# Ups first, downs last: the feed-forward values of a float32 two-block kernel take a detour through HBM

## The reference

```
def conv_ffn(h, up, conv_w, conv_b, down):
    hid = causal_dwconv(h @ up, conv_w, conv_b)
    gate, val = jnp.split(hid, 2, axis=-1)
    return (jax.nn.gelu(gate) * val) @ down

h = rms_norm(x, pre_ffn_norm)
y = conv_ffn(h, up, conv_w, conv_b, down)
x = x + rms_norm(y, post_ffn_norm)
```

## Time and profile before

| what | value |
|---|---|
| median of 3 runs | 2734.21 us (2734.03 to 2734.27) |
| profiled execution: span, first to last instruction | 2732.1 us |
| what lies around the span, as the runs have it | 2.1 us (2734.2 - 2732.1) |
| TensorE matmul busy | 2721.5 us, 100% of the span, 14368 matmuls |
| DVE busy | 1481.2 us, 54% |
| ACT busy | 844.7 us, 31% |
| POOL busy | 192.2 us, 7% |
| mean busy share of the DMA engines | 27.6% on SP's queue, 2.9% on POOL's |
| HBM read / written | 268.41 MB / 16.78 MB |

### The profile page before, as it was taken

The page is one execution under the profiler, slowest core; times in us unless marked ns, Lnnn a source line. Parts: engine busy times, 40 slices in busy tenths (PEclk is TensorE's granted clock), DMA queues, the critical chain, the costliest instruction groups (busy, mean ns, idle before and its releaser), DMA issues.

```text
span 2732.1 us, 34402 instructions
## 1 busy us (share of the span) xinstructions
PE 2721.5 (100%) x14368; PEld 2235.1 (82%) x14368; DVE 1481.2 (54%) x1764; ACT 844.7 (31%) x917; POOL 192.2 (7%) x193
## 2 busy tenths in 40 slices
PE   9999999999999999999999999999999999999998
PEld 8778877877888887789888888888888888888888
DVE  6556567753545665426854444445445453545455
ACT  5345346534412334223421212121222122212215
POOL 1003100530000000010100000000000000000033
PEclk9999999999999999999999999999999999999999
DMA  6225312442222221422422223222322322232242
GB/s 227 90 80 221 111 62 77 162 152 93 98 93 93 93 73 39 154 93 79 168 99 102 93 93 106 95 93 95 106 93 93 102 98 93 94 107 93 93 156 91
DMA packets 46328, 290.39 MB, mean 106 GB/s; under 512 B 5728, under 2 KB 9952, under 8 KB 12784
## 3 DMA queue, kind: packets, MB, share of 16 engines
q1 hardware_dynamic: 40352, 260.22, 27.6%
q0 software_dynamic: 5552, 27.86, 2.9%
q10 hardware_dynamic: 288, 0.27, 0.0%
HBM read 268.41 MB, written 16.78 MB: 104 GB/s over the span
## 4 chain that ended last, share of the span: by engine, by line
PE 98%; DMA 1%; DVE 1%; POOL 0%; ACT 0%; issue 0%; DVEq 0%; ACTq 0%
PE ps L1436 11%; PE ps L1435 11%; PE ps L1437 11%; PE ps L722 10%; PE ps L724 10%; PE ps L723 10%; PE ps L1453 5%; PE ps L1452 5%; PE ps L1451 5%; PE ps L1329 1%; PE ps L1331 1%; PE ps L1330 1%; PE ps L1391 1%; PE ps L1392 1%; PE ps L1393 1%; PE ps L890 1%
## 5 line engine op out<-in xcount | busy, mean ns | idle before, releaser
L1552 ACT ACTIVATE w_hi<-raw 128x2048 fp32r<-128x2048 f32 x225 | 430.7, 1914 | 1136.7 <-PE ps L1437 467.3
L2178 DVE TENSOR_TENSOR w_lo<-raw,w_hi 128x2048 fp32r<-128x2048 f32 x225 | 523.5, 2327 | 455.2 <-ACT w_hi L1552 455.1
L1435 PE MATMUL ps<-h_hi,w_hi 128*128 128x512 f32 x1280 | 497.9, 389 | 0.0
L1436 PE MATMUL ps<-h_lo,w_hi 128*128 128x512 f32 x1280 | 497.9, 389 | 0.0
L1437 PE MATMUL ps<-h_hi,w_lo 128*128 128x512 f32 x1280 | 497.9, 389 | 0.0
L722 PE MATMUL ps<-h_hi,w_hi 128*128 128x512 f32 x1200 | 481.6, 401 | 0.0
L724 PE MATMUL ps<-h_hi,w_lo 128*128 128x512 f32 x1200 | 468.1, 390 | 0.0
L723 PE MATMUL ps<-h_lo,w_hi 128*128 128x512 f32 x1200 | 467.8, 390 | 0.0
L1435 PEld LDWEIGHTS ps<-h_hi,w_hi 128*128 128x128 f32 x1280 | 240.2, 188 | 49.9
L1437 PEld LDWEIGHTS ps<-h_hi,w_lo 128*128 128x128 f32 x1280 | 240.2, 188 | 49.9
L1436 PEld LDWEIGHTS ps<-h_lo,w_hi 128*128 128x128 f32 x1280 | 240.2, 188 | 49.8
(11 more groups left out here) (471 smaller groups left out, 2981.2 us busy)
## 6 DMA issues: line engine op xcount, KB each, us to landing
raw<-weights SPq DMA_DIRECT2D x231, 1024.0 KB, 4.8
x_spill<-X POOLq DMA_DIRECT2D x8, 1024.0 KB, 8.6
x_res<-x_in SPq DMA_DIRECT2D x4, 1024.0 KB, 6.9
x<-X POOLq DMA_DIRECT2D x4, 1024.0 KB, 4.5
x_res<-x SPq DMA_DIRECT2D x4, 1024.0 KB, 7.1
X<-x_spill POOLq DMA_DIRECT2D x4, 1024.0 KB, 9.7
x_back<-x_spill POOLq DMA_DIRECT2D x4, 1024.0 KB, 8.9
out<-y_acc SPq DMA_DIRECT2D x8, 288.0 KB, 2.2
```

The lines of the kernel that those rows point to most:

```text
L1435: pe.matmul(o, w_hi[:, s % 2, w], h_hi[:, t, :], start=(t == 0), stop=False)
L1436: pe.matmul(o, w_hi[:, s % 2, w], h_lo[:, t, :], start=False, stop=False)
L1552: A(w_hi[:, slot, :], raw[:, slot, :], ACT.Copy).then_inc(w_hi_ready, 1)
L2178: V.tensor_tensor(w_lo[:, slot, :], raw[:, slot, :], w_hi[:, slot, :].bitcast(F32), ALU.subtract).then_inc(w_ready, 1)
```

## The change

TensorE now runs up(0) to up(10) first, and then down(0) to down(9) and the last one. `f_hi` and `f_lo` can't hold eleven segments, so the gated values of segments 1 to 10 go to a new HBM tensor, `f_spill`: POOL stores each pair of tiles (512 KB) when DVE has multiplied it, 20 stores in all. In the down phase SP loads a segment (1 MB) into `f_raw`, ACT rounds it to `f_hi` in one instruction, and DVE forms `f_lo` in one. Segment 0 is still rounded at once and kept. `f_raw` lies on the place of `hid`, `f_gate`, `f_val` and `hid_b`; so SP waits for all 20 stores before the first load. The loops of DVE, ACT and SP over the up projections have one segment per turn, and their programs for the down phase are written out without loops. DVE does the multiplication of a segment's second half right after its convolution, at the end of the up projection's program. The weights lie in HBM as before; only the order in which they are loaded changes. `F_STORED` counts on from the stores that were there before.

```diff
--- before.py
+++ after.py
@@ -334,7 +334,9 @@
         f_gate = wf.take("f_gate", [128, 2, S])
         f_val = wf.take("f_val", [128, 2, S])
         hid_b = wf.take("hid_b", [128, 2, 2 + S])
+        f_raw = nc.alloc_sbuf_tensor_at("f_raw", [128, 2, 4, S], F32, offset=W0 + 16 * S * 4)
         AHEAD = U_FFN + 1
+        U_UPS, U_DOWNS = U_FFN + U_UP, U_FFN + U_UP * SEGS
         w_hi_ahead = nc.alloc_sbuf_tensor_at("w_hi_ahead", [128, UNIT], F32R, offset=W0 + 16 * S * 4)
         w_lo_ahead = nc.alloc_sbuf_tensor_at("w_lo_ahead", [128, UNIT], F32R, offset=W0 + 16 * S * 4 + 4 * UNIT)
         x_back = nc.alloc_sbuf_tensor_at("x_back", [128, 16, S], F32, offset=H0)
@@ -441,6 +443,8 @@
         x1 = nc.dram_tensor("x1", (128, KT, S), F32, kind="Internal").ap()
         x_spill = nc.dram_tensor("x_spill", (128, KT, S), F32, kind="Internal").ap()
         x_spill2 = nc.dram_tensor("x_spill2", (128, KT, S), F32, kind="Internal").ap()
+
+        f_spill = nc.dram_tensor("f_spill", (128, FFT, S), F32, kind="Internal").ap()
 
         def par(name, at=0, n=1):
             c = PARAM[name]
@@ -467,6 +471,8 @@
         down_tile = sem("down_tile")
         f_ready = sem("f_ready")
         x_landed = [sem(f"x_landed_{k}") for k in range(4)]
+        f_landed, F_LANDED = x_landed[2:4], 48
+        f_stored, F_STORED = sem("x_spilled"), 192
         dve_order, act_order, pool_order = sem("dve_order"), sem("act_order"), sem("pool_order")
 
         full = {b: sem(f"bank{b}_full") for b in range(4, 8)}
@@ -521,10 +527,28 @@
             for s in range(4):
                 sp.wait_ge(w_ready, U_WO2 + s + 1)
                 sp.dma_start(raw[:, s % 2, :], weights[U_WO2 + s // 2 + 2 * (s % 2)]).then_inc(raw_landed[s % 2], 16)
-            with sp.Fori(U_WO2 // 2 + 2, N_UNITS // 2) as i:
+            with sp.Fori(U_WO2 // 2 + 2, U_UPS // 2) as i:
                 for s in range(2):
                     sp.wait_ge(w_ready, 2 * i + (s + 1))
                     sp.dma_start(raw[:, s, :], weights[2 * i + s]).then_inc(raw_landed[s], 16)
+            with sp.Fori(0, SEGS - 1) as i:
+                for s in range(U_UP):
+                    sp.wait_ge(w_ready, U_UP * i + (U_UPS + s + 1))
+                    sp.dma_start(raw[:, s % 2, :], weights[12 * i + (U_UPS + s)]).then_inc(raw_landed[s % 2], 16)
+            def load_f(seg):
+                sp.dma_start(f_raw[:, seg % 2, :, :], f_spill[:, 4 * seg:4 * seg + 4, :]).then_inc(f_landed[seg % 2], 16)
+
+            for seg in range(SEGS):
+                for q in range(U_DOWN):
+                    sp.wait_ge(w_ready, U_DOWNS + 4 * seg + q + 1)
+                    n = U_UPS + 12 * seg + U_UP + q if seg < SEGS - 1 else N_UNITS - U_DOWN + q
+                    sp.dma_start(raw[:, q % 2, :], weights[n]).then_inc(raw_landed[q % 2], 16)
+                    if (seg, q) == (0, 3):
+                        sp.wait_ge(f_stored, F_STORED + 32 * (SEGS - 1))
+                        load_f(1)
+                    if q == 3 and seg + 2 < SEGS:
+                        sp.wait_ge(f_ready, 2 + seg)
+                        load_f(seg + 2)
             for k in range(8):
                 sp.wait_ge(sem("out_tiles"), k + 1)
                 sp.dma_start(out[:, 2 * k:2 * k + 2, E1], y_acc[:, 2 * k:2 * k + 2, E1]).then_inc(sem("out_stored"), 16)
@@ -637,6 +661,10 @@
             pool.wait_ge(h_ready, 84)
             pool.wait_ge(sq_ready, 96)
             pool.memset(y_acc[:, :, :], 0.0).then_inc(sem("zeroed"), 1)
+            with pool.Fori(0, SEGS - 1) as i:
+                for b in range(2):
+                    pool.wait_ge(sem("f_gated"), 2 * i + (2 + b + 1))
+                    pool.dma_start(f_spill[:, bass.ds(4 * i + (4 + 2 * b), 2), :], f_val[:, :, :]).then_inc(f_stored, 16)
 
             pool.wait_ge(w_used, N_UNITS - U_DOWN - U_DOWN + 1)
             for k in range(4):
...
@@ -1454,11 +1482,10 @@
                         mm.then_inc(w_used if j == 3 else down_tile, 1)
 
             ffn_opening(U_FFN, G_FFN)
-            for i in range((SEGS - 1) // 2):
-                for e in range(2):
-                    u = U_FFN + 8 + 24 * i + 12 * e
-                    ffn_up(u, G_FFN + 4 + 8 * i + 4 * e)
-                    ffn_down(u + 8, 2 * i + e, e)
+            for seg in range(1, SEGS):
+                ffn_up(U_FFN + 8 * seg, G_FFN + 4 * seg)
+            for seg in range(SEGS - 1):
+                ffn_down(U_DOWNS + 4 * seg, seg, seg % 2)
             def sum_half(half):
 
                 def add(x, first, last):
...
@@ -2080,28 +2107,30 @@
                 hi_half(1, t)
 
 
-            def ffn_up(u, pairs, seg, par_):
+            def ffn_up(u, pairs, seg):
                 for s in range(8):
                     if s:
                         step_hi(u, pairs, s)
-                    b = s // 5
                     if s in (2, 6):
-                        act.wait_ge(sem("f_gates"), seg * 2 + (b + 1))
+                        act.wait_ge(sem("f_gates"), seg * 2 + (s // 4 + 1))
                         A(f_gate[:, :, :], f_gate[:, :, :], ACT.Gelu_apprx_tanh).then_inc(sem("f_gelu"), 1)
-                    if s == 4:
-                        round_values(seg, b, par_)
+                step_hi(u + 8, pairs + 4, 0)
 
             def round_values(seg, b, par_):
                 act.wait_ge(sem("f_gated"), seg * 2 + (b + 1))
                 A(f_hi[:, par_, 2 * b:2 * b + 2, :], f_val[:, :, :], ACT.Copy).then_inc(sem("f_hi_ready"), 1)
 
-            def ffn_down(u, pairs, seg, par_):
+            def ffn_down(u, seg):
 
                 for q in range(4):
-                    step_hi(u, pairs, q)
+                    if q:
+                        step_hi(u, u // 2, q)
                     if q == 1:
-                        round_values(seg, 1, par_)
-                step_hi(u + 4, pairs + 2, 0)
+                        nxt = seg + 1
+                        act.wait_ge(f_landed[nxt % 2], F_LANDED + 16 * ((nxt + 1) // 2))
+                        act.wait_ge(w_used, u + 1)
+                        A(f_hi[:, nxt % 2, :, :], f_raw[:, nxt % 2, :, :], ACT.Copy).then_inc(sem("f_hi_ready"), 1)
+                step_hi(u + 4, u // 2 + 2, 0)
 
             for t in range(4, KT):
                 wait_x(52, t)
@@ -2128,11 +2157,10 @@
             A(f_gate[:, :, :], f_gate[:, :, :], ACT.Gelu_apprx_tanh).then_inc(sem("f_gelu"), 1)
             step_hi(U_FFN + 8, (U_FFN + 8) // 2, 0)
             round_values(0, 1, 0)
-            with act.Fori(0, (SEGS - 1) // 2) as i:
-                for e in range(2):
-                    off = 8 + 12 * e
-                    ffn_up(U_FFN + off + 24 * i, (U_FFN + off) // 2 + 12 * i, 2 * i + (1 + e), 1 - e)
-                    ffn_down(U_FFN + off + 8 + 24 * i, (U_FFN + off + 8) // 2 + 12 * i, 2 * i + (1 + e), 1 - e)
+            with act.Fori(0, SEGS - 1) as i:
+                ffn_up(8 * i + U_UPS, 4 * i + U_UPS // 2, i + 1)
+            for seg in range(SEGS - 1):
+                ffn_down(U_DOWNS + 4 * seg, seg)
             def step_hi_end(n):
                 slot = n % 2
                 act.wait_ge(raw_landed[slot], (N_UNITS // 2) * 16)
@@ -3083,24 +3111,33 @@
                 V.tensor_tensor(f_lo[:, par_, 2 * b:2 * b + 2, :], f_val[:, :, :],
                                 f_hi[:, par_, 2 * b:2 * b + 2, :].bitcast(F32), ALU.subtract).then_inc(f_ready, 1)
 
-            def ffn_up(u, seg, par_):
-
-
+            def ffn_up(u, seg):
                 for s in range(8):
                     if s:
                         step_lo(u, s)
+                    if s == 7:
+                        step_lo(u + 8, 0)
+                    b, c = s // 4, s // 2 % 2
                     if s % 2:
-                        ffn_take(u, s, s // 2 % 2)
-                    elif s:
-                        ffn_group(seg, (s - 1) // 4, (s - 1) // 2 % 2, par_)
-
-            def ffn_down(u, seg, before):
+                        ffn_take(u, s, c)
+                    if s in (2, 6):
+                        ffn_group(seg, b, 0, None)
+                    if s in (4, 7):
+                        b = s // 7
+                        dve.wait_ge(f_stored, 32 * seg + (F_STORED + 16 * b - 32))
+                        ffn_group(seg, b, 1, None, finish=False)
+                        dve.wait_ge(sem("f_gelu"), seg * 2 + (b + 1))
+                        V.tensor_tensor(f_val[:, :, :], f_gate[:, :, :], f_val[:, :, :], ALU.mult).then_inc(sem("f_gated"), 1)
+
+            def ffn_down(u, seg):
                 for q in range(4):
-                    step_lo(u, q)
-                    if q == 0:
-                        ffn_group(before[0], 1, 1, before[1], finish=False)
+                    if q:
+                        step_lo(u, q)
                     if q == 1:
-                        ffn_split(before[0], 1, before[1])
+                        nxt = seg + 1
+                        dve.wait_ge(sem("f_hi_ready"), 2 + nxt)
```

(21 more changed lines are left out.)

## The result

| | before | after |
|---|---|---|
| median of 20 runs, us | 2734.19 (2733.71 to 2734.70) | 2738.68 (2738.31 to 2739.24) |
| span of the profiled execution, us | 2732.1 | 2737.0 |

The ratio is 1.0016, with a 95% interval of 1.0010 to 1.0023: the change costs 4.5 us, 0.16%. The forecast was 2737.3, 3.1 us lost. The 4.9 us between the two spans lie in two places: 3.2 at the seam, as forecast, and 1.6 at the end, between the last instruction of the computation and the end of the span, where the prediction had nothing. (The medians differ by 0.4 us less than the spans. The runs lie 1.7 us above the span with the change and 2.1 before.)

What follows compares the result with a forecast made beforehand. The prediction took TensorE's own matmul pace as the bound, in up and down alike. Waits of 1.0 and 2.1 us at the seam made 3.1 on a 2732.1 span, plus 2.1 to the runs: 2737.3 us, range 2735.1 to 2740.5.

Steps and rivals of the forecast that it cites:

- Up phase and nine down segments costed at nothing: Up projections and down segments 1 to 9: spare time of 1.8 and 3.5 us covers the added work, no loss.
- Wait ahead of the second unit: First down segment: DVE's additions now follow the multiplication, at +11.84 instead of before 10.88, so TensorE waits 1.0 us.
- Wait ahead of the third: First down segment: additions stand behind a subtraction needing last store and first load; third unit at 24.8, 2.1 us lost.
- the 12 that the prediction had set as a sign of being wrong: Last store at the seam: issue expected 11.5 us after the first down matmul; later than 12 us would mean wrong.
- the 3 to 4 of the prediction: Last 512 KB store at the seam: expected to land in 3 to 4 us, with 3.4 in the sum.
- The end: Last down segment and kernel end: `x_back` loads released as before, DVE has 3.5 us spare, cost nothing.
- the forecast's 1.8 to 5.4: Whole kernel: the forecast case, 1.8 to 5.4 us lost, chance 0.74.
- A: Seam: transfers are faster or overlap more, only 0 to 1.8 us lost, 2734.2 to 2736.0; chance 0.09.
- B: Seam: TensorE's clock falls in the wait, 5.1 to 7.1 us lost in all, 2739.3 to 2741.3; chance 0.06.
- C: Seam: POOL can't write the store while DVE is busy, 7.5 us lost, 2741.7; chance 0.06.
- D: All matmuls: a distance shorter by 0.001 us on each of 5760 makes it 5.8 us faster; chance 0.03.

Runs made afterwards that it cites:

- e2: Changed kernel with the next segment's rounding and subtraction one down unit later, and the last multiplication behind the first down unit's additions: 2735.51 us, ratio 1.0005.
- e3: Changed kernel with its 20 stores on ACT's queue instead of POOL's: 2736.82 us, ratio 1.0008.
- e1: Changed kernel with ACT's rounding and DVE's subtraction for the next segment in the third down unit instead of the second: 2737.05 us, ratio 1.0009.
- e5: Kernel before the change plus 20 unneeded POOL stores of 128 KB just ahead of the feed-forward loop: 2735.96 us, ratio 1.0006.

## Why the prediction was right, and what it missed

**Up phase and nine down segments costed at nothing:** right. No wait of TensorE there.

**Wait ahead of the second unit, 1.0 forecast:** 1.25. The multiplication ended 11.40 after the first down matmul (forecast 11.2); the idle 0.28 ahead of the convolution stood in no row of before. In e2, where this segment stands outside DVE's loop, the convolution starts 0.11 after the tiles are taken. The addition and its handover add 0.73 (forecast 0.63).

**Wait ahead of the third, 2.1 forecast:** 1.68, for a total of 2.93 against 3.1. The third unit starts at +24.82; the forecast was 24.8. Two steps were mis-sized and cancelled. POOL's issue came at +12.05 instead of 11.5, past the 12 that the prediction had set as a sign of being wrong. Of this, 0.2 is the later multiplication; the rest is that POOL issued 0.65 us behind it (0.66 to 0.71 at all 20 stores), where I had taken 0.3 from a store with a fixed address. Here POOL also computes the address after its wait, but these two instructions are over 0.13 us behind the multiplication, and ACT in e3 computes the address too and needs 0.17 in all; the other 0.5 no run explains. And the store of 512 KB landed in 2.9, below the 3 to 4 of the prediction and its 3.4, which I had set between the earlier trace rows. The load's 4.8, the rounding's 1.92 and the subtraction's 2.29 held. The chain was the right one; that the third unit's start fits to 0.02 us is luck.

**No cost of a restart:** I had none; there are 0.13 us for each of the two waits. With them the seam costs 3.2.

**"The end. ... I cost it at nothing":** the step that failed. I asked there what the loads of `x_back` and DVE's instructions would do, and not what ended last. The 20 stores were costed as hidden because their queue had nothing to do. That held for each store, and not for their sum at the end: 20 times 0.082 = 1.6 us of POOL's drain, on the path. The earlier trace rows show those last 7 us with no engine busy for more than 0.74 of them, and I read only the clock there, not who was waited for. With this term the forecast would have been 2737.3 + 1.6 = 2738.9, against 2738.68. It comes that near because small things cancel again: the two restarts and 0.1 ahead of the loop were not in the sum, and the 2.1 from span to median was 1.7. The measured 4.5 us lie within the forecast's 1.8 to 5.4, but over a third of them has a cause that the forecast did not name.

**The rivals.** A (the cover holds) fell: the chain came too late by what was worked out. B (the clock falls) fell: 1.00 in the slice of the seam, through waits of 1.25 and 1.68 us with 11 us of work between. It was less safe than I took it to be. I set a wait of 2.1 against the 4 us after which the clock fell in the earlier trace rows; at the end of the changed kernel it fell 2.1 us after the last matmul. The seam did not come to the test, since the longest wait was 1.68. So the Trainium skill's rule on oscillation ("TensorE: Matmul & The Clock Gate", "HAM oscillation — how this bites in real kernels") did not come into play at waits of 1.25 and 1.68 us; whether it would have at 2.1 no run shows. C (the store is held back by a busy DVE) fell: the multiplication and four additions and a w_lo ran without a gap from 2242.6 to 2248.4, and the store, issued at 2244.49 amid the additions, landed in 2.9 like all 20. In e2 the last store is issued at 2246.17, while a w_lo runs (2245.43 to 2247.71), and lands in 2.9 too. The lock-out that "SBUF — State Buffer" ("SBUF: two separate sides") of the Trainium skill warns of did not show with these instructions. D (shorter distance) fell: 0.2266 us before and after.

## What to carry to other kernels

When a loop over A, B is split into all A, then all B with a detour through HBM, look at the seam alone: the last store and the first load stand in a row there, and what an in-order engine holds ahead of urgent work because of them is what is paid. Move the wait behind the urgent work (e1, e2) and it is free. And read which engine ends last before costing added transfers at nothing: here each one that POOL issues lengthens the end of the kernel, whether it stands 1400 us before the end (e5) or 500.

## What the runs showed of the hardware that I had not expected

- POOL's last drain takes 7.642, 9.19 and 10.83 us with 61, 80 and 100 transfers issued by POOL, that is 0.082 us for each, for 16, 128 or 512 KB alike. Its first 2.57 us pass beside POOL's last two additions. What it does in the time behind them no run shows.
- A store of 512 KB by POOL lands in 2.9 us, 20 of 20 times; by ACT's queue the median is 2.6. A store of POOL whose address a loop computes is issued 0.66 us after its producer's end, with a fixed address 0.30; by ACT, with a computed address, 0.17.
- The first matmul after a wait of 1.25 or 1.68 us lasts 0.47 instead of 0.39, and the restart costs 0.13 us, at an unchanged granted clock.
- The clock's step down behind TensorE's last matmul came 4.0 us after it in the kernel before and 2.1 us after it with the change.
- DVE's w_lo lasts 3.16 us (2651.28 in the changed kernel) beside POOL's multiplications of `x_back`, and 2.29 without them.
